# New-state products next to scores, one output product moved, and values ahead of turns in a three-block transformer kernel

## The reference

```
def step(state, xs):                       # one block of 32 tokens
    qd, ke, vv, dec = xs
    o = einsum('blhd,bhde->blhe', qd, state)
    state = dec[..., None] * state + einsum('blhd,blhe->bhde', ke, vv)
    return state, o
...
s = einsum('bqhgd,bjhd->bhgqj', q_c, k_c) * scale    # scores
p = softmax(s)                                       # with sinks or a bias
o = einsum('bhgqj,bjhd->bqhgd', p, v_c)              # values
```

## Time and profile before

| | before |
|---|---|
| median of the runs | 1053.11 us |
| the profiled execution | 1053.4 us |
| its span, first to last instruction | 1051.6 us |
| busy: TensorE, VectorE, ScalarE | 99%, 70%, 60% |
| mean granted TensorE clock | 1.000 |

### The profile page before, as it was taken

How to read it: one execution, slowest core, us unless ns; L and a number is a source line. 1 busy time by engine, 2 the same in 40 slices (tenths; PEclk the granted TensorE clock), 3 DMA queues, 4 the chain that set the end, 5 groups by cost and what they waited for, 6 DMA issues and landing times.

```text
span 1051.6 us, 16501 instructions
## 1 busy us (share of the span) xinstructions
PE 1041.5 (99%) x6536; PEld 915.2 (87%) x6536; DVE 740.3 (70%) x1114; ACT 633.7 (60%) x1089; POOL 118.1 (11%) x143
## 2 busy tenths in 40 slices
PE   8999999999999999999999999999999999999998
PEld 6988989888888898798888888889889989888887
DVE  6787775998846577759888555957656885666751
ACT  5767756776734577557767444447876655655630
POOL 4121000131100000001111000221110000111100
PEclk9999999999999999999999999999999999999999
DMA  7753447665664855366656656455543655665651
GB/s 263 285 171 116 160 141 263 197 191 173 209 192 139 295 163 163 111 231 205 195 178 208 196 176 216 154 204 172 165 137 121 182 158 201 194 190 178 214 187 41
DMA packets 57116, 192.80 MB, mean 183 GB/s; under 512 B 6856, under 2 KB 9808, under 8 KB 57040
## 3 DMA queue, kind: packets, MB, share of 16 engines
q1 hardware_dynamic: 57040, 191.76, 56.9%
HBM read 190.67 MB, written 1.06 MB: 182 GB/s over the span
## 4 chain that ended last, share of the span: by engine, by line
PE 93%; DVE 3%; POOL 1%; ACT 1%; issue 1%; DMA 1%; DVEq 0%; ACTq 0%; POOLq 0%
PE ps L1020 29%; PE ps L1109 20%; PE ps L1101 15%; PE ps L1110 10%; PE ps L1381 5%; PE ps L1252 3%; PE ps L1168 2%; PE ps L1178 2%; PE ps L1189 2%; PE ps L1121 1%; DVE lo L1569 1%; PE ps L1237 1%; PE ps L1439 1%; PE ps L1291 1%; POOL hr L591 1%
## 5 line engine op out<-in xcount | busy, mean ns | idle before, releaser
L1569 DVE TENSOR_TENSOR lo<-raw,hi 128x1024 fp32r<-128x1024 f32 (+2 forms) x347 | 431.1, 1265 | 89.1 <-ACT hi L655 86.3
L655 ACT ACTIVATE hi<-raw 128x1024 fp32r<-128x1024 f32 (+2 forms) x347 | 347.4, 1036 | 93.6 <-DMA raw<-in_weights 87.6
L1109 PE MATMUL ps<-y_both,hi 128*128 128x512 f32 x912 | 310.7, 389 | 0.0
L1110 PE MATMUL ps<-y_both,lo 128*128 128x256 f32 x912 | 251.8, 276 | 0.0
L1109 PEld LDWEIGHTS ps<-y_both,hi 128*128 128x128 f32 x912 | 171.2, 188 | 35.3
L1110 PEld LDWEIGHTS ps<-y_both,lo 128*128 128x128 f32 x912 | 171.2, 188 | 0.0
L1101 PE MATMUL ps<-y_both,hi 128*128 128x256 f32 x784 | 138.3, 280 | 0.8 <-DVE lo L1569 0.8
L1101 PEld LDWEIGHTS ps<-y_both,hi 128*128 128x128 f32 x784 | 118.9, 188 | 3.8 <-issue 2.6
L1101 PE MATMUL ps<-y_both,lo 128*128 128x256 f32 x392 | 108.8, 278 | 0.0
L1020 PE MATMUL ps<-hi,y_both 128*128 128x512 f32 x352 | 94.2, 382 | 2.9 <-DVE lo L1569 1.4
L1020 PE MATMUL ps<-hi,h_hi 128*128 128x512 f32 x294 | 91.0, 391 | 0.0
(11 more groups left out here) (292 smaller groups left out, 1396.7 us busy)
## 6 DMA issues: line engine op xcount, KB each, us to landing
raw<-in_weights SPq DMA_DIRECT2D x331, 512.0 KB, 4.2
gain<-in_gains SPq DMA_DIRECT2D x10, 512.0 KB, 7.4
raw<-in_weights SPq DMA_DIRECT2D x8, 384.0 KB, 7.2
bias<-in_rel SPq DMA_DIRECT2D x16, 128.0 KB, 2.2
raw<-in_weights SPq DMA_DIRECT2D x8, 256.0 KB, 2.6
mem_x<-in_mem SPq DMA_DIRECT2D x2, 512.0 KB, 9.4
h<-in_x SPq DMA_DIRECT2D x2, 256.0 KB, 2.7
h<-in_x SPq DMA_DIRECT2D x1, 512.0 KB, 6.1
```

The costliest lines, as they stand in the source:

```text
L655: act.activation(hi_at(n)[:, :w], raw_at(n)[:, :w], ACT.Copy).then_inc(hi_done, 1)
L1109: pe.matmul(dst, hi_at(n)[:, at], y_both[:, :, k, :], start=k == 0, stop=False)
L1110: mm = pe.matmul(dst[:, 0:S], lo_at(n)[:, at], y_hi[:, k, :], start=False, stop=k == KD - 1)
L1569: dve.tensor_tensor(lo_at(n)[:, :w], raw_at(n)[:, :w], hi_at(n)[:, :w].bitcast(F32), ALU.subtract).then_inc(lo_done, 1)
```

## The change

In the first layer `kv` moves from behind `turn_probs` to directly behind `scores`, the third pair of blocks moves from step 2 to step 3 and the seventh block from step 3 to step 5 (and to the other bank, since the first output of the recurrence is still in its old one). VectorE does both updates of a pair back to back, ahead of the inverse of the sums. `hgrn` of the first half waits for five states rather than seven. In the output projection the group (0, 1) moves from behind (3, 0) to behind (7, 0). In the second layer and the third block the values (`mix_pair`, `mix_heads`) stand ahead of the turns.

```diff
+        KV_AT = {0: (0, 1), 1: (2, 3), 3: (4, 5), 5: (6,)}
+
         def kv_bank(b):
 
-            return (7, 5)[b % 2]
+            return (7, 5)[b % 2 or b // 6]
...
             def kv(blocks):
 
-                for b in blocks:
-                    if b >= 2:
-                        pe.wait_ge(stated, b - 1)
+                if blocks[0] >= 2:
+                    pe.wait_ge(stated, blocks[0])
...
                     scores("a", s + 2)
+                if s in KV_AT:
+                    kv(KV_AT[s])
                 if s % 2 and s >= 3:
                     mix_pair("a", (s - 3) // 2)
                 if s:
                     turn_probs("a", s - 1)
-                if s < 4:
-                    kv((2 * s, 2 * s + 1) if s < 3 else (6,))
                 if s in (4, 6):
-                    pe.wait_ge(stated, 7)
+                    pe.wait_ge(stated, (5, 7)[s // 6])
...
             for u in range(1, 4):
                 even_part(u, 0)
-            pe.wait_ge(fill_evac, 6)
-            pe.wait_ge(y_lo_done, 4 * 2 + 3)
-            even_part(0, 1)
             for u in range(4, 8):
                 if u == 6:
                     pe.wait_ge(y_lo_done, 4 * 2 + 4)
                 mm = even_part(u, 0)
             mm.then_inc(tile_done, 1)
-            for u in range(1, 8):
+            pe.wait_ge(fill_evac, 6)
+            for u in range(8):
                 if u == 6:
                     turn_normed(3, 4, 0)
                 even_part(u, 1)
...
-                if j >= 2:
-                    turn_pair(j - 2)
                 if j >= 3:
                     if j in (7, 9):
                         pe.wait_ge(y_lo_done, 4 * 5 + (j - 5) // 2)
                     mix_pair("c", j - 3)
+                if j >= 2:
+                    turn_pair(j - 2)
...
-                if k:
-                    turn_pairs(k - 1)
                 if k in (6, 8):
                     pe.wait_ge(br_lo, k // 2 - 2)
                 if k >= 2:
                     mix_heads(third_heads(k - 2))
+                if k:
+                    turn_pairs(k - 1)
                 gate_unit(k + 2)
-            turn_pairs(9)
             pe.wait_ge(br_lo, 3)
             mix_heads(third_heads(8))
+            turn_pairs(9)
...
-                if 0 <= s < 4:
-                    new_state(2 * s)
+                for b in KV_AT.get(s, ()):
+                    new_state(b)
...
                 if s < 7:
                     sinks_inverse(s + 1)
-                if 0 <= s < 3:
-                    new_state(2 * s + 1)
```

## The result

The changed kernel took 1057.59 us in the median of four runs (1057.48 to 1057.93); the kernel before, beside it on the same chip, 1052.67 us. The ratio is 1.0048, with a 95% interval of 1.0036 to 1.006: slower by about 5 us, where 1058.5 was predicted, inside the range. The profiled execution took 1057.48 us, its span is 1055.7 us (1051.6 before), and the mean granted clock is 0.996 (1.000 before).

The account below looks back on a forecast made before the run. TensorE, busy 99% of the span, was taken to bound the kernel. Terms 5.5 + 2.5 - 2.1 - 0.5 = +5.4 us on the profiled 1053.4 gave 1058.8, a median of 1058.5 us; range 1054.0 to 1060.6 us.

Parts of the forecast that it names:

- The moved product: First layer's output projection: moving (0,1) delays a weight load, so TensorE waits longer before tile 0's turn; +5.5 us.
- The clock: Behind that wait of about 6.1 us TensorE resumes at the lower clock level; +2.5 us, bounds 0 to 2.8.
- Values ahead of turns: Second layer and third block: twelve steps each 0.175 us shorter through a cheaper tile-shape switch; -2.1 us.
- New-state products next to scores: First layer's loop: shorter wait for the state update, most gain taken back by ScalarE at the sixth step; -0.5 us.
- The sum: Whole kernel: all four terms together, +5.4 us against the profiled execution, predicted median 1058.5 us.
- the clock stays up: Rival: no clock fall in the wait before tile 0's turn; +2.9 us, 1056.0 us, chance 0.22.
- the load does not decide: Rival: tile 0's norm starts earlier on its finished products, the wait goes; 3.2 us gained, 1049.9 us, chance 0.10.
- the orders bring nothing: Rival: every border in the reordered loops still costs its switch; +7.5 us, 1060.6 us, chance 0.06.
- the stall is half as long and the clock stays: Rival: half the wait before tile 0's turn, no clock fall; within 0.2%, about 1053.5 us, chance 0.07.

Follow-up runs that it names:

- e7: Kernel before, with only values put ahead of turns in the second layer and third block: 1050.52 us, ratio 0.9976.
- e1: Changed kernel with output product (0,1) back in its old place behind (3,0), all else as changed: 1050.13 us, ratio 0.9972.
- e6: Kernel before, second layer's steps reordered to values, turns, scores, projections, with as many tile-shape switches as before: 1054.16 us, ratio 1.0008.
- e2: Kernel before with only output product (0,1) moved behind (7,0): 1060.43 us, ratio 1.0072.
- e5: Changed kernel with output product (0,1) behind (5,0), two groups later than before instead of four: 1054.18 us, ratio 1.0009.
- e4: Changed kernel with ten unused products of ones added on TensorE ahead of the turn of tile 0: 1055.4 us, ratio 1.0023.
- e3: Changed kernel, but ScalarE and VectorE take two units of the next stage, not three, ahead of tile 0's norm: 1049.35 us, ratio 0.9965.
- e8: e3 with ScalarE's copy emptying the projections' bank ahead of its other work in the first layer's fifth step: 1049.22 us, ratio 0.9964.

## Why the prediction was right

- **The moved product** (predicted +5.5, measured +5.0). The load was issued 0.02 us behind the 48th product, and the wait came where it was put, released by VectorE's scaling. The half microsecond less is the load: it landed in 3.53 us rather than 3.99, the term for which the bounds of 5.0 to 6.0 had been kept. With the product in its old place the load landed in 3.65 to 3.99 us (e7, e1, e6 and before), with the product moved in 3.46 to 3.73 (e2, changed, e5, e4). Part of the half microsecond is thus the spread of single landings; whether a late load lands sooner these few traces do not settle. e5 and e2 show that it counts group by group; e3 shows the link that makes it count, the order on ScalarE and VectorE.
- **The clock** (predicted +2.5, measured +1.6). The mechanism was right; this is the term that was mis-sized. It was taken near the start of the span, where the lower level lasts 5.5 us of work. Here the level had already fallen inside the wait, at about 147, and was back at 154, so only some 3.5 us of work ran at it, and about half of that was lost. e4 takes away this term alone.
- **Values ahead of turns** (predicted -2.1, measured -2.27 in the trace, -2.5 by e7's ratio with some 0.9 us of uncertainty either way). The switch is not paid at another border: the steps shrank by 0.17 us. e6 refutes that the gain came from having the values earlier.
- **New-state products next to scores** (predicted -0.5, measured -0.55). The wait went from 0.75 to 0.23 us, 0.2 having been foreseen, and ScalarE's run took back the rest, at the step that the prediction named. That the number agrees so closely is partly luck: the projections of that step started 0.35 us earlier, not 0.5, and the other 0.2 us came behind it, unforeseen. e8's reordering inside that run did not move this limit. No run has this part of the change alone; e1 less e7 leaves 0.4 us for it, with more than 1 us of uncertainty, so it rests on the rows.
- **The sum.** +5.4 was predicted against the profiled execution, +4.1 measured: 0.5 less for the landing, 0.9 less for the clock, 0.2 more gained in the loops and the first layer, and 0.3 more ahead of the first layer's loop, which is within the spread of single executions. The median came out at +4.9, nearer to the prediction than the single execution; that difference lies within the spread of single executions.
- **The rivals.** That the clock stays up is refuted by the windows after. That the load does not decide is refuted for this change, but e3 makes it true with two short edits, and its 1049.35 us stands beside the 1049.9 that the rival gave. That the orders bring nothing is refuted by e1 and e7. That the stall is half as long and the clock stays is refuted by the wait of 5.56 us and the windows; e5 shows what half the distance gives, 2.90 us.

What stays open: e3 and e8 leave a wait of 0.4 to 0.5 us at the sixth step; whether a shorter run on ScalarE would remove it was not tried.

## What to carry to other kernels

Where a ring of buffers feeds an engine, the last use of a slot is also the issue of a later load: before moving a use, look up which load takes its slot and what stands queued behind the work on that load, even if that work itself is not urgent. If a move delays such a load, look first whether the waiting engines need it at that point in their order; here a change of one unit in that order turned a loss of 5 us into a gain of 3.7. Order products so that neighbours share a tile shape, count the borders of a step, and price one by the same instruction with either kind of neighbour.

## What the runs showed of the hardware that had not been expected

- In these traces, one for each kernel, the clock's price did not grow with the wait. Waits of 0.34 us (e1) and 1.44 us (e4) left the granted clock at 1.00; 2.90 us (e5) cost 1.6 us of slow work, 5.48 and 5.56 us (e2 and the changed kernel) 1.8 and 1.6.
- In e5 the fall came after the wait, not in it: the turn ran at the full clock and the products behind it at half. So the engine can be seen busy and slow behind a gap that is already over.
- The clock also fell once without a wait of the kind studied here: in e6's profile it is 0.58 and 0.57 in the windows from 14 to 16 and 16 to 18 us, far ahead of the edit, and TensorE is busy throughout both:

```profile
14.00:16.00 2.00, 2.00 (x7) 1.68 (x8) 2.00 (x4) 0.28 (x1) 0.00 (x0) 0.58 1.03 412
```

The first layer's loop starts at 72.1 us there, 0.5 to 1.8 later than in the other traces. Ahead of the fall TensorE had waited 1.45 us (up to 13.86), but so it does in the other nine traces, 1.30 to 1.45 us, and there the clock stays at 1.00. What brought the fall is open. It may not be rare: of the 27 executions of the kernel before that were timed with e6, five had a mean clock of 0.998, and they were the five slowest (1053.87 to 1054.37 us, the median being 1053.18). None of these was traced.
